# Feed-forward up products by Strassen's scheme in half blocks, with hidden groups of 512 features

## The reference

```python
def _sq_relu_mlp(h, w1, w2):
    return jnp.square(jax.nn.relu(h @ w1)) @ w2
...
h2 = _rms_norm(x, norm_mlp[l]) * (1.0 + sc2) + sh2
x = x + g2 * _sq_relu_mlp(h2, w_mlp1[l], w_mlp2[l])
...
return _rms_norm(x, norm_final)
```

## Time and profile before

| what | value |
|---|---|
| median of 3 runs | 1625.81 us (1625.06 to 1625.85) |
| the profiled execution's own time | 1626.04 us |
| its span, first to last instruction | 1624.3 us |
| PE busy | 1607.9 us, 99% of the span |
| weight loads busy | 1336.6 us, 82% |
| DVE, ACT, POOL busy | 829.1, 680.8, 583.0 us (51%, 42%, 36%) |
| mean granted clock of TensorE | 0.999 of full speed |

### The profile page before, as it was taken

The page is one execution under the profiler, slowest core; times in us unless marked ns, Lnnn a source line. Parts: engine busy times, 40 slices in busy tenths (PEclk is TensorE's granted clock), DMA queues, the critical chain, the costliest instruction groups (busy, mean ns, idle before and its releaser), DMA issues.

```text
span 1624.3 us, 20270 instructions
## 1 busy us (share of the span) xinstructions
PE 1607.9 (99%) x8308; PEld 1336.6 (82%) x8308; DVE 829.1 (51%) x1239; ACT 680.8 (42%) x1043; POOL 583.0 (36%) x289
## 2 busy tenths in 40 slices
PE   9999999999999999999999999999999999999998
PEld 6888898889888878888887767789878788888887
DVE  7787867676665364443443646681356621111112
ACT  6533343443432433555455463423435643332323
POOL 1002113221344434334333434353323465555542
PEclk9999999999999999999999999999999999999999
DMA  6453333343355223233223241122112133222221
GB/s 234 153 204 131 125 127 134 116 132 121 133 205 207 104 91 104 93 103 103 94 90 121 78 156 66 52 87 73 53 40 78 65 117 104 91 103 92 98 85 52
DMA packets 53252, 179.16 MB, mean 110 GB/s; under 512 B 6428, under 2 KB 7068, under 8 KB 52776
## 3 DMA queue, kind: packets, MB, share of 16 engines
q1 hardware_dynamic: 53160, 177.88, 31.5%
HBM read 172.58 MB, written 2.12 MB: 108 GB/s over the span
## 4 chain that ended last, share of the span: by engine, by line
PE 92%; DVE 5%; ACT 1%; issue 1%; DMA 0%; SPq 0%; POOL 0%; DVEq 0%; ACTq 0%; POOLq 0%
PE banks L427 90%; PE banks L430 2%; DVE ACC L1182 1%; DVE wl L1146 1%; ACT T L1969 0%; DMA maskf<-cst_dram 0%; DVE ada L1130 0%; DVE X L1130 0%; ACT wh L1972 0%; ACT Sc L1969 0%; DVE ML L1130 0%; DVE T L1912 0%; ACT L1969 0%; DVE Sc L1130 0%; DVE E L1912 0%
## 5 line engine op out<-in xcount | busy, mean ns | idle before, releaser
L2553 POOL TENSOR_TENSOR wl<-raw,wh 128x1024 fp32r<-128x1024 f32 x171 | 424.2, 2485 | 525.3 <-ACT wh L1972 525.3
L427 PE MATMUL banks<-HH,wh 128*128 128x512 f32 (+1 forms) x1040 | 413.2, 397 | 2.6 <-ACT T L1969 0.9
L427 PE MATMUL banks<-HL,wh 128*128 128x512 f32 (+1 forms) x1040 | 402.3, 390 | 0.3 <-DVE HL L1130 0.3
L1972 ACT ACTIVATE wh<-raw 128x1024 fp32r<-128x1024 f32 x246 | 257.0, 1052 | 296.9 <-PE banks L427 289.0
L427 PE MATMUL banks<-HH,wl 128*128 128x512 f32 x1032 | 282.6, 390 | 0.0
L427 PEld LDWEIGHTS banks<-HH,wh 128*128 128x128 f32 (+1 forms) x1040 | 194.9, 187 | 50.0 <-issue 5.5
L427 PEld LDWEIGHTS banks<-HL,wh 128*128 128x128 f32 (+1 forms) x1040 | 194.7, 187 | 42.0 <-issue 1.4
L427 PEld LDWEIGHTS banks<-HH,wl 128*128 128x128 f32 x1032 | 193.4, 188 | 41.5 <-issue 1.0
L427 PE MATMUL banks<-wh,HH 128*128 128x256 f32 x448 | 128.5, 287 | 0.0
L427 PE MATMUL banks<-wl,HH 128*128 128x256 f32 x448 | 126.7, 283 | 0.0
L427 PE MATMUL banks<-wh,HL 128*128 128x256 f32 x448 | 126.6, 283 | 0.0
(11 more groups left out here) (354 smaller groups left out, 2627.5 us busy)
## 6 DMA issues: line engine op xcount, KB each, us to landing
raw<-wst_dram SPq DMA_DIRECT2D x294, 512.0 KB, 3.2
X<-xT_dram SPq DMA_DIRECT2D x8, 512.0 KB, 6.6
CB<-sums_dram SPq DMA_DIRECT2D x12, 256.0 KB, 3.1
D<-dec_dram SPq DMA_DIRECT2D x12, 256.0 KB, 2.8
out_dram<-XT SPq DMA_DIRECT2D x8, 256.0 KB
QS<-QX SPq DMA_DIRECT2D x24, 64.0 KB, 2.6
KSw<-KX SPq DMA_DIRECT2D x24, 64.0 KB, 2.0
MX<-memT_dram SPq DMA_DIRECT2D x2, 512.0 KB, 8.7
```

The lines of the kernel that those rows point to most:

```text
L427: return pe.eng.matmul(dst, w, x, start=start, stop=stop, skip_group_check=True)
L1972: return eng.activation(dst, src, ACT.Copy)
L2553: tt(wl[:, q, :], raw[:, i % NRAW, :], wh[:, q, :].bitcast(F32), ALU.subtract).then_inc(*by_pool("low", u))
```

## The change

Up units 4 to 15 (of 16) are computed by a scheme of Strassen's kind. The unit's 256 features are two halves of 128, the 512 tokens two halves of 256, and the 4 steps of k of a tile two halves of 2. Of the eight products of half blocks seven remain, on sums of blocks: four blocks of sums are formed from each weight tile (`WS`, then high and low parts `SH_`, `SL_`), four from the activations, once (`XS`, `XSH`, `XSL`, from `XW` = high + low). Each product is 6 matmuls of 256 columns. The seven results lie in banks 2 to 5 and DVE and ACT add them up (`PS`); relu and square become one DVE instruction (`hidden`). These units' tiles have the kind "s".

The groups of hidden features become eight of 512. The order is up 0, up 1, and then, for each further unit, the unit and two down tiles of the group before. A down unit is now one tile (4 k), so X is added to twice as often. `DVE_LOW` gains every second down tile, and in the groups from 2 on POOL makes all `FLO`. The bytes loaded are the same.

```diff
+FF = [("up", 0), ("up", 1)]
+for _g in range(1, 8):
+    for _h in range(2):
+        FF += [("up", 2 * _g + _h), ("down", _g - 1, 2 * _h), ("down", _g - 1, 2 * _h + 1)]
+FF += [("down", 7, _n) for _n in range(4)]
+SEVEN = 4
...
+    for step in FF:
+        if step[0] == "up":
+            pair("up", 0, 8, (256 * step[1],), "s" if step[1] >= SEVEN else "w")
+        else:
+            pair("down", 4 * step[1], 4 * step[1] + 4, (256 * step[2],))
...
+NS = 3
+DVE_LOW = frozenset([*range(73), 164, *(u for u, w in enumerate(w for w in PLAN if w[0] != "ada")
+                                        if w[1] == "down" and w[3][0] % 512)])
...
# tensor, a unit of seven products
+                def product(b, c, a, x):
+                    o, s0 = bank[b][:, 256 * c:256 * c + 256], kh == 0 and c == 0
+                    for q in range(2):
+                        mm(o, a[0][:, q, :], x[0][:, q, :], s0 and q == 0, False)
+                        mm(o, a[0][:, q, :], x[1][:, q, :], False, False)
+                    for q in range(2):
+                        i = mm(o, a[1][:, q, :], x[0][:, q, :], False, kh == 1 and q == 1)
+                    return i
+                pe.wait_ge(done("high", w), done("low", w), done("x sums", kh), *free[2])
+                product(2, 0, of_w(1, 0), of_x(1, 0))
+                product(2, 1, of_w(0, 0), of_x(0, 0)).then_inc(*by_pe("seven", u, kh, 0))
+                pe.wait_ge(done("sums high", w), done("sums low", w), *free[3])
+                product(3, 0, of_w(1, 1), of_t(3))
+                product(3, 1, of_s(2), of_t(1)).then_inc(*by_pe("seven", u, kh, 1))
+                pe.wait_ge(*free[4])
+                product(4, 0, of_s(1), of_t(0))
+                product(4, 1, of_s(0), of_t(2)).then_inc(*by_pe("seven", u, kh, 2))
+                pe.wait_ge(*free[5])
+                product(5, 0, of_s(3), of_x(1, 1)).then_inc(*by_pe("seven", u, kh, 3))
+                by_pe.also("w free", w)
...
+        def down(g, n):
+            u = feed.take()
+            pe.wait_ge(*(done("l", "f", g, k) for k in range(4)))
+            features(("down", g, n), FHI[g % 2], FLO[g % 2], range(4), True, True, (0, 1), u)
...
# vector, in split(i, u)
+            if PLAN[i][0] == "s":
+                v = S_AT[u]
+                w, s = blocks(raw[:, i % NRAW, :]), WS[:, v % 2, :].rearrange("p (s q c) -> p s q c", s=4, q=2)
+                dve.wait_ge(done("raw", i), done("sums low", S_TILES[v - 2]) if v > 1 else done("l", "f", 0, 1))
+                tt(s[:, 0:2, :, :], w[:, 0, :, :, :].rearrange("p q i c -> p i q c"), w[:, :, :, 1, :],
+                   ALU.subtract).then_inc(*by_dve())
+                dve.wait_ge(by_dve.last())
+                tt(s[:, 2, :, :], w[:, 1, :, 1, :], s[:, 0, :, :], ALU.add).then_inc(*by_dve())
+                dve.wait_ge(by_dve.last())
+                tt(s[:, 3, :, :], w[:, 1, :, 0, :], s[:, 2, :, :], ALU.subtract).then_inc(*by_dve("summed", i))
...
# vector: x_sums(kh) is 4 instructions of 512 elements, x_sums_low(kh) 2 of 1024
+        def seven(u):
+            g, n = u // 2, 2 * (u % 2)
+            kept = done("kept", ("up", u - 1), 0) if u > SEVEN else None
+            dve.wait_ge(done("seven", u, 1, 1), done("first product", u), kept)
+            tt(PS[:, 1, :], bank[3][:, 256:512], PS[:, 0, :], ALU.add).then_inc(*by_dve())
+            dve.wait_ge(done("seven", u, 1, 2), by_dve.last())
+            tt(PS[:, 2:4, :], psum[:, 4, :].rearrange("p (a c) -> p a c", a=2), PS[:, 1:2, :].to_broadcast([128, 2, 256]),
+               ALU.add).then_inc(*by_dve())
+            t = turn("hidden", g, n + 1)
+            dve.wait_ge(by_dve.last(), temp_free("hidden", g, n + 1))
+            tt(t[:, :].rearrange("p (a c) -> p a c", a=2), psum[:, 3:5, 0:256], PS[:, 3:4, :].to_broadcast([128, 2, 256]),
+               ALU.add).then_inc(*by_dve("kept", ("up", u), 1))
+            hidden(g, n + 1, t)
+            t = turn("hidden", g, n)
+            dve.wait_ge(done("seven", u, 1, 3), temp_free("hidden", g, n))
+            tt(t[:, :].rearrange("p (a c) -> p a c", a=2), psum[:, 2:6:3, 0:256], PS[:, 0:3:2, :],
+               ALU.add).then_inc(*by_dve("kept", ("up", u), 0))
+            hidden(g, n, t)
+        def hidden(g, k, t):
+            dve.wait_ge(by_dve.last())
+            stt(t[:, :], t[:, :], 0.0, t[:, :], ALU.max, ALU.mult).then_inc(*by_dve("f", g, k))
...
+            if u == 2:
+                x_sums(0)
+            if u == 3:
+                x_sums_low(1)
+        def down(g, n):
+            feed.take()
...
+            if (g, n) == (0, 0):
+                x_sums_low(0)
+            if (g, n) == (0, 1):
+                x_sums(1)
...
# scalar, in split(i, u)
+            if PLAN[i][0] == "s":
+                v = S_AT[u]
+                act.wait_ge(done("summed", i), done("w free", S_TILES[v - NS]) if v >= NS else None)
+                copy(SH_[:, v % NS, :], WS[:, v % 2, :]).then_inc(*by_act("sums high", u))
...
# gpsimd, in split(i, u), and in up(u)
+            if PLAN[i][0] == "s":
+                v = S_AT[u]
+                pool.wait_ge(done("sums high", u))
+                tt(SL_[:, v % NS, :], WS[:, v % 2, :], SH_[:, v % NS, :].bitcast(F32), ALU.subtract).then_inc(*by_pool("sums low", u))
...
+            if u in (1, 2):
+                for k in range(4 * u - 4, 4 * u):
+                    x_whole(k)
```

More of the change, by code:

```diff
@@ L1933, in down @@
-        def down(g):
-            for n in range(4):
-                feed.unit()
-                for j in range(2):
[L1937 to L1948, removed]
@@ L1955, in vector @@
+        for step in FF[1:]:
+            (up if step[0] == "up" else down)(*step[1:])
         dve.wait_ge(done("root"))
@@ L2507, in down @@
-        def down(g):
-            for n in range(4):
-                feed.unit()
-                for j in range(2):
[L2511 to L2530, removed]
+        def x_sums_high(kh):
+            for n in range(2):
+                act.wait_ge(done("x summed", kh, n))
+                copy(XSH[:, kh, 2 * n:2 * n + 2, :, :], XS[n][:, :, :, :]).then_inc(*by_act("x sums high", kh, n))
+        def up(u):
+            feed.unit()
+            g = u // 2
+            if u >= SEVEN:
+                act.wait_ge(done("seven", u, 1, 0), done("kept", ("up", u - 1), 0) if u > SEVEN else done("x sums", 1))
+                copy(PS[:, 0, :], bank[2][:, 256:512]).then_inc(*by_act("first product", u))
+                for k in (2 * (u % 2) + 1, 2 * (u % 2)):
+                    high(g, k, temp("hidden", g, k))
+                return
+            for j in range(2):
+                k = 2 * (u % 2) + j
+                t = temp("hidden", g, k)
+                act.wait_ge(done("unit", ("up", u), j), temp_free("hidden", g, k))
+                fn(t[:, :], bank[j + 2 * (u == 1)], ACT.Relu).then_inc(*by_act("relu", g, k))
+                by_act.also("kept", ("up", u), j)
+                high(g, k, t)
+            if u == 1:
+                for j in range(2):
+                    high(g, j, E[j])
+            if u == 2:
+                x_sums_high(0)
@@ new lines, in down @@
+        def down(g, n):
+            if (g, n) == (7, 0):
+                fn(sm[:, 0:1], one, ACT.Sqrt).then_inc(*by_act())
+            feed.take()
+            for j in range(2):
+                t, m = 2 * n + j, done("kept", ("down", g, n), j)
+                if g == 7 and t == 7:
+                    q = temp("last", "x5")
+                    act.wait_ge(temp_free("last", "x5"))
+                    for h in range(2):
+                        c = slice(256 * h, 256 * h + 256)
+                        act.wait_ge(done("last tile", h))
+                        fn(q[:, c], X[:, t, c], ACT.Square).then_inc(*by_act("last square half", h))
+                elif g == 7:
+                    square("x5", t, X[:, t, :], T, m)
+                if g == 7:
+                    act.wait_ge(m, done("seven", 15, 1, 3))
+                    fn(XG[:, t, :], X[:, t, :], ACT.Copy, scale=P("gfin", t)).then_inc(*by_act("weighted", t))
+            if (g, n) == (0, 1):
+                x_sums_high(1)
@@ L2686, in low, with x_whole, up @@
                 return True
[L2688 to L2705, removed]
+        def x_whole(k):
+            pool.wait_ge(done("h", "x4", k), done("l", "x4", k))
+            tt(XW[:, k, :], HH[:, k, :].bitcast(F32), HL[:, k, :].bitcast(F32), ALU.add).then_inc(*by_pool("x whole", k))
+        def up(u):
+            feed.unit()
+            g = u // 2
+            for k in (1, 0) if u >= SEVEN else (0, 1):
+                k += 2 * (u % 2)
+                if low(g, k, temp("hidden", g, k)):
+                    by_pool.also("temp", turns["hidden", g, k])
+            if u == 1:
+                for j in range(2):
+                    low(g, j, E[j])
+            if u in (1, 2):
+                for k in range(4 * u - 4, 4 * u):
+                    x_whole(k)
+        for step in FF[1:]:
+            if step[0] == "up":
```

(3 more changed lines are left out.)

163 lines of the change are left out of this document (88 added, 75 removed).

## The result

The changed kernel took 1696.38 us (median of 4 runs, 1695.12 to 1697.84) where the kernel before took 1625.83 on the same chip (1625.06 to 1626.95): a ratio of 1.0435, 95% interval 1.0422 to 1.0448. It is slower, as forecast, but by 70.6 us and not by 24.3, and lies above the range.

A forecast was written before the change was run, and what follows sets the result against it. TensorE's own work was taken to bound the kernel. Saving -9.6, way in +13 and second-down-tile stalls +20.9 gave +24.3 us on 1626.04: 1650.3 us (span near 1648.6), range 1632 to 1682.

The forecast's parts named there:

- 24 x 0.40 = 9.6 us saved: TensorE, units 4 to 15: 24 tiles of seven products take 5.04 us each in place of 5.44, saving 9.6 us.
- cycle 20.96: Steady cycle of one unit's two "s" tiles and two down tiles on TensorE: 10.08 + 10.88 = 20.96 us.
- DVE and POOL exclude each other: A DVE instruction with both inputs in SBUF and a POOL instruction block each other; excluding parts 20.3 of 20.96 us.
- The place where it hurts: Second down tile waits for DVE's X addition, which stands behind the weight sums: 1.9 us late, 11 times, 20.9 us.
- The walk undisturbed: DVE's instructions followed from the unit's last matmul without blocking: X addition ends at 5.25 us, due at 5.44.
- First sum (no dependence) to 3.60: DVE's first weight sum follows the second hidden at once, ending at 3.60 us; POOL's first FLO gets in only then.
- POOL gets in earlier: Rival: FLO precedes the second hidden; 4.1 us a cycle, 16 at the start, +51.5, 1677.5 us; chance 0.25.
- the bound of 4.1: Upper stall per cycle if POOL precedes the second hidden or first sum, so a whole wl precedes the third sum.
- The way in: Three stalls before the steady cycle, taken as 6, 2 and 5 us, together 13, bounds 5.4 and 16.
- Nothing for the rest: DMA, raw buffers, starting relu waits and the last bank's tail add nothing; the last four tiles at most 1 us.

The follow-up runs named there:

- experiment 4: The changed kernel with POOL's FLO left out from group 2 on, so its output lacks the right low parts: 1633.72 us, ratio 1.0052 against the kernel before.
- experiment 6: The changed kernel with POOL's two FLO of each seven-product unit made after its work for the next down tile, nothing left out: 1636.39 us, ratio 1.0066.
- experiment 5: The changed kernel with the two semaphore waits of the first weight sum moved ahead of the second hidden: 1703.31 us, ratio 1.0474.
- Experiment 2: The changed kernel with 28 spare matmuls of 256 columns ahead of the second down tile at all twelve stalls: 1675.88 us, ratio 1.0311.
- experiment 3: The changed kernel with groups of 512 only, no unit using the seven products and no sums of X: 1627.65 us, ratio 1.0012.
- (1): The changed kernel with DVE's additions of a first down tile into X put ahead of the weight sums: 1639.54 us, ratio 1.0087.

## Why the prediction was right or wrong

- **"24 x 0.40 = 9.6 us saved", cycle 20.96: right.** Seven products run at the pace of the earlier trace rows, and a cycle without stalls takes 20.98 (experiment 4).
- **DVE and POOL exclude each other: right.** Sums of 0.69 and 0.42 us take 1.79, 1.39 and 2.44 in the profile after, and 0.69, 0.42 and 0.43 once no `FLO` is there (experiment 6). X additions and bank additions, which read PSUM, keep their 0.75 and 0.69.
- **"The place where it hurts", the second down tile, 11 times: right.** The walk undisturbed comes to 5.10 against 5.25.
- **"First sum (no dependence) to 3.60": wrong, the first step that failed.** I had read from the eight instructions of the earlier trace rows that "DVE instructions that follow without a dependence let nobody in". In this cycle POOL got in after the second `hidden`, with no dependence between it and the sum, and experiment 5 shows it again with no semaphore wait between the two. Then the rest came as the walk goes from there: `FLO`, `FLO`, and the whole `wl` ahead of the third sum, 3.74 us where the rival "POOL gets in earlier" had 4.1 and I took 1.9. This is worth 11 x (3.74 - 1.9) = 20.2 us. Counted as the prediction counts, the lateness is 3.9 against its 4.1. That rival, with 0.25 of chance, had the size, but not for the reason that it gave: it hung on `FLO` being ready ahead of the second `hidden`, and `FLO` came 0.10 after it had started. What happened is the other case of the bound of 4.1, "or the first sum". With its own sum of 1677.5 the rival would still have been 19 us short, for the reason in the next point.
- **A term that the sum didn't have: TensorE's clock behind a stall.** The stall was priced at its own length. 28.1 us came on top: 21.9 of clock at the 1.2 GHz level in the 11 cycles, 3.3 between the recorded idle time and the delay that it makes, and 2.9 at the first waits. Experiment 2 confirms the size: 20.5 of them go when TensorE is kept busy in the same stalls. This is the largest error.
- **The way in: right in its waits.** 6 + 2 + 5 = 13 against 5.91 + 1.67 + 4.21 = 11.8, each at its place. The clock behind the first and the last of them is in the point above.
- **"Nothing for the rest": right.** No wait of size stands elsewhere, and the groups of 512 by themselves cost 0.12% (experiment 3).

Together: 20.2 + 28.1 - 1.2 = 47.1, which is the distance of the spans, 1695.7 against 1648.6.

What stays open: why eight DVE instructions in a row kept POOL out in the earlier trace rows and two don't here. Who asked first doesn't explain it: that `wl` is recorded from 984.11 on, half a microsecond ahead of the first of the eight. Those eight are one operation repeated with both inputs in SBUF; whether that matters wasn't tried. Nor is it shown why the clock stayed up behind two of the twelve stalls.

## What to carry to other kernels

Ahead of giving DVE and POOL work that each would hide, look at what stands in the same program ahead of the instruction that the bounding engine waits for; here one moved call (1) or two moved operations (6) were worth 57 to 60 us, and no engine had less to do. When DVE and POOL exclude each other, price the case that the waiting one gets in at every boundary between two instructions, one after another in turn, each time for its whole length; it did so in all 11 cycles here, though not in the earlier trace rows. And price a stall of TensorE at more than its length: here a stall of 3.74 us made the cycle 6.0 longer on average (26.99 against 20.98), and 4.0 where the clock stayed up.

## What the runs showed of the hardware that was not expected

- A waiting POOL instruction got in between two DVE instructions that don't depend on each other: the later one started at 1387.11 and took 1.79 us for 0.69 of work. In experiment 5, with no semaphore wait between the two either, the one at 1415.94 took 1.80.
- Equal stalls of 3.74 us have unequal effects on the clock: 0.50 in the 5 us behind the one that ended at 1393.6, 1.00 behind the one that ended at 1503.5. With 28 matmuls of 256 columns in the stall it was 1.00 in the window of 28 us, and the kernel 20.5 us faster.
- A shorter wait can have it too: behind 1.81 us in experiment 4 the clock was 0.50 from 1314 to 1316, behind 1.50 us in the same place of the changed kernel 1.00.
